# The sums of the attention weights over halves of the keys move from VectorE to GpSimd

## What is computed

```python
# grouped-query heads (latent heads: the same, with two terms in s)
s = jnp.einsum('bkgqd,bskd->bkgqs', qi, k, preferred_element_type=F32) * scale
p = jax.nn.softmax(s, axis=-1).astype(v.dtype)
return jnp.einsum('bkgqs,bskd->bkgqd', p, v)
```

## Time and profile before

| | |
|---|---|
| time, median of 3 runs | 1500.31 us (1497.65 to 1500.95) |
| time of the profiled execution | 1497.4 us, its span 1495.4 us |
| PE busy (matmul) | 1385.5 us, 93% |
| DVE busy | 919.3 us, 61% |
| ACT busy | 569.5 us, 38% |
| POOL busy | 547.8 us, 37% |
| mean granted TensorE clock | 0.977 |

### The profile page before, as it was taken

How to read it: one execution, slowest core, us unless ns; L and a number is a source line. 1 busy time by engine, 2 the same in 40 slices (tenths; PEclk the granted TensorE clock), 3 DMA queues, 4 the chain that set the end, 5 groups by cost and what they waited for, 6 DMA issues and landing times. The chain is left out here.

```text
span 1495.4 us, 14534 instructions
## 1 busy us (share of the span) xinstructions
PE 1385.5 (93%) x5599; PEld 1006.5 (67%) x5599; DVE 919.3 (61%) x945; ACT 569.5 (38%) x803; POOL 547.8 (37%) x263
## 2 busy tenths in 40 slices
PE   5999988887999999999979997988979999999997
PEld 3677643355788888778746784433748888887885
DVE  4766876556678878721176778654467887874212
ACT  4422344443543443422242325344344434433322
POOL 2312331015444444444452215210354444444444
PEclk8999999998999999999989999999989999999997
DMA  7212310012233333233241223000213333332331
GB/s 243 87 29 64 78 30 15 0 39 74 71 99 90 94 99 94 86 89 99 83 141 45 69 53 76 15 0 0 84 51 90 99 91 93 99 97 79 102 92 67
DMA packets 205469, 112.46 MB, mean 75 GB/s; under 512 B 15239, under 2 KB 202361, under 8 KB 204506
## 3 DMA queue, kind: packets, MB, share of 16 engines
q1 hardware_dynamic: 205402, 111.54, 25.8%
HBM read 105.63 MB, written 2.10 MB: 72 GB/s over the span
## 5 line engine op out<-in xcount | busy, mean ns | idle before, releaser
L473 POOL TENSOR_TENSOR wl<-raw,wh 128x1024 fp32r<-128x1024 f32 x184 | 445.9, 2425 | 761.1 <-ACT wh L547 761.1
L547 ACT ACTIVATE wh<-raw 128x1024 fp32r<-128x1024 f32 x184 | 194.9, 1059 | 593.4 <-PE ps L957 553.9
L955 PE MATMUL ps<-gh,wh 128*128 128x512 f32 (+1 forms) x896 | 362.7, 405 | 7.5 <-POOL wl L473 7.5
L956 PE MATMUL ps<-gl,wh 128*128 128x512 f32 (+1 forms) x896 | 354.1, 395 | 0.0
L957 PE MATMUL ps<-gh,wl 128*128 128x512 f32 (+1 forms) x896 | 354.0, 395 | 0.0
L955 PEld LDWEIGHTS ps<-gh,wh 128*128 128x128 f32 (+1 forms) x896 | 167.9, 187 | 52.9 <-issue 13.6
L956 PEld LDWEIGHTS ps<-gl,wh 128*128 128x128 f32 (+1 forms) x896 | 167.9, 187 | 43.8 <-issue 4.1
L957 PEld LDWEIGHTS ps<-gh,wl 128*128 128x128 f32 (+1 forms) x896 | 167.9, 187 | 41.1
L1777 DVE SCALAR_TENSOR_TENSOR cv<-pad,pm,cv 128x512 f32<-128x512 f32 x88 | 130.4, 1482 | 83.3 <-ACT cv L857 83.3
L1367 DVE TENSOR_TENSOR acc<-acc,sq 128x512 f32<-128x512 f32 x24 | 60.7, 2531 | 192.4 <-ACT sq L591 192.2
L955 PE MATMUL ps<-fh,wh 128*128 128x512 f32 x352 | 139.1, 395 | 3.3 <-POOL wl L473 3.3
(11 more groups left out here) (243 smaller groups left out, 1910.6 us busy)
## 6 DMA issues: line engine op xcount, KB each, us to landing
raw<-w_up SPq DMA_DIRECT2D x88, 512.0 KB, 3.8
raw<-w_down SPq DMA_DIRECT2D x32, 512.0 KB, 4.0
raw<-w_in SPq DMA_DIRECT2D x30, 512.0 KB, 4.0
raw<-w_out SPq DMA_DIRECT2D x16, 512.0 KB, 4.1
raw<-w_down SPq DMA_DIRECT2D x16, 384.0 KB, 3.4
xio<-x SPq DMA_DIRECT2D x4, 512.0 KB, 4.5
win<-c_win SPq DMA_DIRECT2D x2, 1024.0 KB, 4.9
TF<-c_tf SPq DMA_DIRECT2D x2, 1024.0 KB, 9.5
```

The source lines that it names most:

```text
L473: nc.gpsimd.tensor_tensor(wl[:, slot, :], raw[:, slot, :], wh[:, slot, :].bitcast(F32), ALU.subtract).then_inc(S["lo_ready"], 1)
L547: A(wh[:, slot, :], raw[:, slot, :], ACT.Copy).then_inc(S["hi_ready"], 1)
L955: mm(ps[0:cols, bank, :], w_hi, x_hi, start=start and k == 0, stop=False)
L956: mm(ps[0:cols, bank, :], w_hi, x_lo, start=False, stop=False)
```

## The change

DVE's `row_sums` is taken out of DVE's list, and the same addition, with the same waits, is put into POOL's list: for h from 1 to 11 the sum of head h - 1 stands behind `shift(h)` and `q_lo(h + 1)`, and the sum of head 11 at the end of the loop.

```diff
@@ block of gpsimd
+                def row_sums(h):
+                    pool.wait_ge(S["p_ready"], lay * N_TILES + (h + 1) * TC)
+                    if h >= 2:
+                        pool.wait_ge(S["den_mm"], lay * PAIRS + h // 2)
+                    pT = probT[h % 4]
+                    nc.gpsimd.tensor_tensor(tsum[:, h % 2, :, :], pT[:, 0:2, :], pT[:, 2:4, :], ALU.add).then_inc(S["summed"], 1)
...
                         q_lo(h + 1)
                         pool.wait_ge(S["q2lo"], lay * GH + h + 2)
+                    row_sums(h - 1)
+                row_sums(HEADS - 1)
@@ block of vector
-                def row_sums(h):
-                    dve.wait_ge(S["p_ready"], lay * N_TILES + (h + 1) * TC)
-                    if h >= 2:
-                        dve.wait_ge(S["den_mm"], lay * PAIRS + h // 2)
-                    pT = probT[h % 4]
-                    tt(tsum[:, h % 2, :, :], pT[:, 0:2, :], pT[:, 2:4, :], ALU.add).then_inc(S["summed"], 1)
...
-                    if h:
-                        row_sums(h - 1)
...
                     if h == 11:
                         pair_out(PAIRS - 2)
-                        row_sums(HEADS - 1)
                         group_norm(1)
```

## The result

The changed kernel takes 1533.03 us (median of 4 runs, 1530.24 to 1536.48), the kernel before beside it on the same chip 1500.63 us (4 runs, 1497.65 to 1502.30). The ratio is 1.0224, with an interval of 1.0198 to 1.0249: slower by 32.4 us. Forecast were 1529 us, slower, within 1515 to 1536.

The account below looks back on a forecast made before the run. PE was taken to bound the kernel. Per layer, relief -2.0, stalls +11.4, absorbed -1.3, collisions +4.15, clock +2.2 gave +14.45, 28.9 for both: 1497.4 to 1526.3 us, plus 2.9 to the median, 1529 us; range 1515 to 1536.

Parts of the forecast that it names:

- The wait that moves: Even heads' sums on POOL wait for denominators, delaying `shift` and `q_lo`: +4.4 us at heads 3, 5; +1.3 at 7, 9.
- The addition on POOL: One sum on POOL takes 2.40 us, with bounds of 2.1 and 2.5 us.
- Relief: Three PE holes behind DVE's sums close, at 217.19 (0.90), 227.53 (0.72) and 235.35 (0.37): -2.0 us per layer.
- The third hole: PE's hole of 0.37 us at 235.35, following a DVE held up by a sum, closes.
- Collisions: DVE and POOL take turns: +1.0 us at head 5, +1.4 at head 9, +1.75 at head 11; +4.15 per layer.
- The clock: PE's clock falls behind the stalls of heads 3 and 5: 1.1 us each, 2.2 us per layer.
- 1.3 absorbed: Behind head 5's stall, PE's hole of 1.31 us at 244.29, waiting for Hyena squares, is absorbed: -1.3 us.
- Heads 7 and 9: Stalls of +1.3 us each, with nothing taken for the clock despite 3.3 us of emptiness.
- +1.4: At head 9, DVE's two `yl` take turns with POOL's sum, delaying the maxima of head 11: +1.4 us.
- What is outside: Behind the stage of heads all work is gated by PE, and nothing there absorbs a shift.
- 28.9: Forecast total added in the stage of heads, both layers together, in us.
- 14.45: Forecast total added in the stage of heads of one layer, in us.

Follow-up runs that it names:

- experiment 1: Changed kernel with each sum on POOL placed one head later; 1503.84 us, ratio 1.0039 to the kernel before.
- experiment 8: Changed kernel with sums 0 and 1 at head 2, sums 2 to 9 one head later, 10 and 11 on DVE; 1499.81 us, ratio 0.9999.
- experiment 2: Changed kernel with each addition on POOL made twice, one behind the other; 1571.52 us, ratio 1.0488 to the kernel before.
- second profile: Changed kernel run and profiled once more, unchanged; 1531.80 us, span 1529.8.
- experiment 3: Changed kernel with 12 or 10 unused PE products at the first tile of heads 4, 6, 8 and 10; 1525.65 us, ratio 1.0175.
- experiments 5: Kernel before, with DVE's sums of heads 0 to 9 one head later and behind the maxima; 1498.96 us, ratio 0.9999.
- experiment 6: Kernel before with only odd heads' sums moved to POOL, one head later than in the changed kernel; 1508.03 us, ratio 1.0050.
- experiment 7: Changed kernel with the sums of heads 10 and 11 back on DVE; 1533.66 us, ratio 1.0226 to the kernel before.

## Why the prediction held

It named the cause, and the total, 1529 us, came out 4 us too low. Its steps one by one:

- **The wait that moves** is shown. The stall is 4.27 us at head 3, 4.8 at head 5 with its collision (4.3 without), and 1.26 to 1.32 at heads 7 and 9 (forecast 4.4, 5.4 with the collision, and 1.3), the sum released by the denominators, `shift` right behind it. The waits of PE themselves are shorter than I wrote (2.9 and 0.6 us at head 3, 2.5 at heads 7 and 9, for 3.3, 1.3 and 3.3); the offsets are what the sum is made of, and they hold. The reverse holds too: without that wait, 26 of the 32 us go (experiment 1), the half clock behind the stalls among them, and the whole loss goes when the remaining collisions and the end are avoided as well (experiment 8). A second addition adds its length once per stall (experiment 2).
- **The addition on POOL**: 2.35 us for 2.40.
- **Relief**: right in size, 0.96 at 217.19. The third hole, 0.37 at 235.35, was put down to a sum; it is there without one. The time came back instead at the pair behind 227.53, which had begun with a hole and took 1.10 us and now takes 0.74.
- **Collisions**: the instructions are stretched in every place named. At head 5 the chain grew by 4.80 - 4.27 = 0.5 us, not 1.0: the copy stretched `shift` by 0.19 and the addition `q_lo` by 0.32, and the copy itself waited 0.4 behind the sum. At the end the term was 1.28 for 1.75. There PE waits for `tsum` first (2.0 us), and the wait for `yl` shrinks from 1.38 to 0.6; 2.0 - 0.8 = 1.2 is the gain of one over the other.
- **The clock** is the mis-sized term. Forecast: 1.1 us behind each of two stalls. Behind head 3 the offset rises from 4.04 to 5.91 (at the product that was at 226.21 before) in the second profile, 1.9 us, before the closed holes give some back. Behind head 5 it is 0.8 + 1.3 absorbed = 2.1 us. So 4.0 in place of 2.2: the model was the six products around head 1, but here half clock lay on 10 or more.
- **Heads 7 and 9**, where I took nothing for the clock: behind head 9 it fell in both profiles, behind head 7 in one. Behind head 9 half clock and the split `yl` do not add. PE at half clock reaches the maxima late enough not to wait (1.44 and 1.55 us); at full clock it waits for them (0.87 us, experiment 3). The table's agreement with +1.4 is a right number for a partly wrong reason.
- **What is outside**: I took the rest of the kernel as gated by PE and shifted only. 3.9 and 5.3 us arose there in the two profiles, in part as half clock behind the stage (1.6 and 1.5 us in the second), and some 3 of them are the distance of the profiled execution of the kernel before from its median. What separates the 32.4 us between the medians from 28.9 is thus 1 to 2 us outside the stages, and the falls in head 6 and behind head 7 in those executions that have them. That is argued from two profiles, not shown for the medians, and it isn't settled what decides whether the clock falls at a given one of these places.

In the second profile collisions that I took too large and a clock that I took too small cancel: 14.6 against 14.45 per layer is better than its parts, and that is luck.

## What to carry to other kernels

Before work goes to an idle engine, ask what its first wait is and what stands behind it: an in-order queue passes a late signal on to every instruction behind, and 24 additions that fit four times into the idle time of GpSimd cost 32 us, most of it by one wait, 6 us when each stands one head later, and nothing that can be measured when in addition the last two of a layer stay on VectorE and the others keep clear of VectorE's instructions. Check next which instructions of both vector engines start on one signal. If a closed hole brings no time, look at the granted clock behind the next hole before calling the relief false.

## What the runs showed of the hardware

- A hole of 1.95 us in PE's work in head 6 is followed by full clock in both layers in both profiles of the kernel before and in that of experiment 1, and by a mean clock of 0.79 over 8 us in those of experiments 5 and 8. The changed kernel shows either in its two profiles. Such a stretch costs 1.3 us, nearly the 1.4 of relief of a layer. Less waiting ahead of the hole doesn't explain it: experiment 6, with 1.1 us more waiting there than the kernel before, has the fall too, and experiment 7 has it in layer 1 and not in layer 2. What decides is open.
- Products that nobody uses, 44 per layer, made a kernel 7.4 us faster, 24 per layer made another one 6.5 us faster, and the same 24 in the kernel before changed nothing clear of noise (1.0 us).
- GpSimd and VectorE take turns on these SBUF operations, one instruction at a time. A GpSimd addition of 128 by 1024 takes 2.35 us alone and 2.7 to 3.38 against VectorE; a VectorE subtraction of 128 by 512 takes 0.68 alone and 2.85 to 2.87 behind such an addition. The turns are not always full: at head 5 of the changed kernel the sum ended at 248.91, and a copy of 0.43 us alone and a `shift` of 1.04 alone were both done by 250.09, 0.3 us sooner than one behind the other.
